# A layer with seven-product matrix pairs: the three fp32r passes of a product become the outer loop in every pair

## The chip, the cores and the metric

The kernel runs on one core of a Trainium2 chip. The metric is the device time of one execution in microseconds (us); three executions were timed. All tensors are fp32; a matmul reads its operands as fp32r (fp32 rounded to fewer bits), and a product of full width is built from three fp32r matmuls.

## The reference

One inference step of one layer on 512 prompt tokens and 8 sequences of 8 sample tokens (576 tokens, width 2048):

```python
h = rmsnorm(x, norm_g)
proj = h @ w_in          # merge gates ga, gb; conv inputs cB, cC, cx, cg; q, k, v, gg; rank-16 code
za = cB * causal_conv3(cC * cx) * silu(cg)
zb = head_rmsnorm(gated_linear_attention(q, k, v, code)) * silu(gg)
merged = sigmoid(ga) * (za @ w_branch_a) + sigmoid(gb) * (zb @ w_branch_b)
y = rmsnorm(x + merged @ w_out, final_norm_g)
```

Returned are y for prompt and samples, and the new states of the convolution and of the attention.

## The kernel before

**Two parts.** Up to about 703 us the kernel normalises x and does the k, q, v columns and the attention (its matmuls have line 1620). From there on all matmuls of line 1979 belong to 76 **pairs**. A pair is two 128-column tiles of weights against all 576 tokens and all 2048 rows, worked as a 2x2 block product with 7 sub-products instead of 8 (`PRODUCTS`, `NPROD` = 7): the blocks are a11, a12, a21, a22 of the weights and 288-token halves of the activations.

**The stages.** Pairs 0 to 51 (`FIRST`) are the columns of w_in that are left; pairs 52 to 59 (from `PAIR_A`) are w_branch_a, 60 to 67 (from `PAIR_B`) w_branch_b, 68 to 75 (from `PAIR_C`) w_out. The activation operands of the seven products are the same for all pairs of a stage. They lie in `SLOTS[stage]`: names y11, y12, y21, y22 are quarters of `act_y` (row k of a slot starts 1152 elements after row k - 1), numbers 0 to 3 are slots of `act_x` (row k starts 288 elements after row k - 1, right where row k - 1 ends). Products that read `act_x` are called x products here, the others y products. Stage 1 has four x products in a pair, A three, B four, C three.

**One product** is 8 rows k (`KH`) times 3 passes: 24 matmuls of 128 x 128 weights by 288 columns, added in one PSUM area. The passes (`PASSES`, line 471) are high weights by high activations (0, 0), high weights by low activations (0, 1), low weights by high activations (1, 0). ACT makes the high weights of product g (`split_hi`, line 1158, `ring_hi`, semaphore `part_hi`), DVE then subtracts them from the fp32 weights for the low ones (`split_lo`, line 2099, `ring_lo`, semaphore `part_lo`). Both run two products ahead, in a ring of three (`RING`). Before that, DVE forms the weight sums that four of the seven products need (`add_pieces`, line 2106). After a product ACT or DVE reads the PSUM area (`save`, line 1390, semaphore `part_saved`, and the stage functions such as `out_pair`).

**The order of matmuls** is written out in the PE part (lines 1927 to 1984). In the first pair of a stage (`late`: pairs 0, 52, 60, 68) the pass is the outer loop and k the inner, with passes in the order (0,0), (1,0), (0,1): the low activations are awaited last there, and `part_lo` in front of the second pass. In all other pairs k is the outer loop and the pass the inner, and PE waits for `part_lo` before the first matmul of the product:

```python
late = u in (0, PAIR_A, PAIR_B, PAIR_C)
if not late:
    pe.wait_ge(part_lo, g + 1)
order = [(n, k) for n in range(3) for k in range(KH)]
if not late:
    order = [(n, k) for k in range(KH) for n in range(3)]
```

In stage C PE also turns the finished tiles of the pair before (five transposes of line 1882 in front of products 1 and 3, `turn_out`).

**The end.** In the last pair the products run in `LAST_ORDER` = 0, 1, 2, 4, 5, 3, 6. `turn_early` (four transposes) stands in front of loop step (n, k) = (0, 3) of product 3, and `turn_first_late` (three) in front of (0, 5) of product 6; `turn_late` comes after everything. `turn_early` waits for the sums that DVE makes of products 4 and 5 (`out_pair`, lines 2800 and 2803), `turn_first_late` for that of product 3. DVE adds the turned tiles to the rows of x (`add_last`, line 2821), multiplies rows by the final norm weights (`weight`, line 2841; each call increments `weighted`), ACT squares them (`squares`, line 1453), both make the inverse root (`means`, `root_out`, `roots`), and `scale_row` on ACT (tiles 4 and 2) and DVE (tiles 3, 0, 1) scales the rows, which SP and POOL store. `EARLY` is tiles 3 and 4, `LATE` tiles 0 to 2.

Of the kernel before, what the change touches and what calls it, by code (L numbers as in the profile page):

```python
# [67 lines left out]
PAIRS_G, PAIRS_B, PAIRS_O = len(FIRST), 8, 8  # L68
# [27 lines left out]
def hybrid_kernel(nc, x_prompt, x_sample, state_conv, state_gla, norm_g, w_in, conv_w, w_alpha2,  # L96
# [51 lines left out]
    with ctx:  # L148
# [461 lines left out]
        def place(m):  # L610


            return (m + 1) % PLACES
# [502 lines left out]
        def _(act):  # L1116
# [348 lines left out]
            def save_c21(u):  # L1465

                act.wait_ge(prod_done, NPROD * u + NPROD)
                act.wait_ge(c11_read, u + 1)
                A(mix[u % 2][:, 1, 0:HALF], psum_of(u)[1], ACT.Copy, scale=-1.0).then_inc(c21_act, 1)
# [77 lines left out]
            def scale_row(t, count):  # L1547

                act.wait_ge(y_rstd, count)
                act.wait_ge(weighted, PAIRS_O - 1 + count)  # L1550
                if count == 1:
                    act.wait_ge(back_in, 16 * AWAY)
                for n, (_, part) in enumerate(parts_of_row(t)):
                    if n == 1 and count == 1:
                        save_c21(NPAIR - 1)
                    A(part, part, ACT.Copy, scale=stat[:, 24 + t:25 + t]).then_inc(y_act, 1)


# [12 lines left out]
        def _(pe):  # L1571
# [355 lines left out]
            for u in range(NPAIR):  # L1927
                f = phase_of(u)
                b1, b2, b3 = psum_of(u)
                for g in range(u * NPROD, (u + 1) * NPROD):  # L1930
                    p = product_at(g)
                    slot = SLOTS[f][p]
                    out = (b2, b3, b2, b1, b2, b3, b2)[p]

                    fresh = 0
                    if u == 0 and p in (1, 2, 4, 6):
                        fresh = (1, 2, 4, 6).index(p) + 1
                    if u in (PAIR_A, PAIR_B) and p in AHEAD[f - 1]:
                        pe.wait_ge(blk_in[p], 16 * (f + sum(p in AHEAD[n] for n in range(f))))
                    elif u in (PAIR_A, PAIR_B):  # L1940
                        fresh = split_count(f - 1, p)
                    if u == PAIR_C:
                        fresh = c_split(C_HI, p)
                        if p in SPLIT_WAY:
                            pe.wait_ge(blk_in[p], landed(p))
                    if fresh:
                        pe.wait_ge(x_hi, fresh)
                    if p == 0 and u < U_X and u % 16 == 15:
                        turn_tails(u // 16)
                    if u > PAIR_C and g % NPROD in (1, 3):  # L1950
                        turn_out(u - 1, g % NPROD // 2)
                    if p == 0 and u >= 2:
                        pe.wait_ge(*c21_done(u - 2))
                    if p == 1 and u >= 2:
                        pe.wait_ge(*c12_done(u - 2))
                    if p == 3 and u >= 2:
                        pe.wait_ge(c11_read, u - 1)
                    if p in (2, 4, 5, 6):
                        pe.wait_ge(part_saved, 4 * u + {2: 1, 4: 3, 5: 3, 6: 4}[p])
                    pe.wait_ge(part_hi, g + 1)  # L1960
                    r = g % RING

                    late = u in (0, PAIR_A, PAIR_B, PAIR_C)
                    if not late:
                        pe.wait_ge(part_lo, g + 1)
                    order = [(n, k) for n in range(3) for k in range(KH)]
                    if not late:
                        order = [(n, k) for k in range(KH) for n in range(3)]
                    for n, k in order:
                        if g == NG - 2 and (n, k) == (0, 3):  # L1970
                            turn_early()
                        if g == NG - 1 and (n, k) == (0, 5):
                            turn_first_late()
                        a, b = ((0, 0), (1, 0), (0, 1))[n] if late else PASSES[n]
                        if late and k == 0 and n == 1:
                            pe.wait_ge(part_lo, g + 1)
                        if late and k == 0 and n == 2 and fresh:
                            pe.wait_ge(x_lo, fresh)
                        mm = nc.tensor.matmul(out, (ring_hi, ring_lo)[a][r][:, k * P:(k + 1) * P],  # L1979
                                              slot_of(slot, b)[:, k, :],  # L1980
                                              start=(p in (0, 1, 3) and k == 0 and n == 0),
                                              stop=(k == KH - 1 and n == 2),
                                              skip_group_check=(p in (2, 4, 5, 6)))
                    mm.then_inc(prod_done, 1)
# [5 lines left out]
        def _(dve):  # L1990
# [855 lines left out]
            for u in range(NPAIR):  # L2846
                kind = kind_of(u)
                last = kind_of(u - 1) if u else "branch"
                for p in range(NPROD):
# [58 lines left out]
                    m = u - 1 - PAIR_C  # L2908
                    if m >= 0 and p in (1, 3):
                        add_rows(m, p // 2)  # L2910
                    if u == NPAIR - 1 and p == 5:
                        dve.wait_ge(x_row_in[place(L)], 64 * (L // PLACES + 1))
                        add_last(EARLY, 0, 2, acc[1][:, 0:4 * P], 2 * L + 1)
                    if m >= 0 and p == (6 if u < NPAIR - 1 else 5):
                        weight(m, range(NT + 1), m + 1)
                    if u == NPAIR - 1 and p == 5:
                        means(EARLY, PAIRS_O, L + 1)


            def roots(tiles, count):  # L2920

                dve.wait_ge(rms_out, count)
                refined(of_tiles(16, tiles), of_tiles(8, tiles), None, of_tiles(24, tiles), of_tiles(32, tiles))
                dve.sem_inc(y_rstd, 1)

            def scale_row(t, count):

                dve.wait_ge(weighted, L + count)
                inverse = stat[:, 24 + t:25 + t]
                for n, (_, part) in enumerate(parts_of_row(t)):  # L2930
                    at = place(L) if n == 2 else part.shape[1]
                    ins = V.tensor_scalar(part[:, 0:at], part[:, 0:at], inverse, None, ALU.mult)
                    if n == 2:
                        last = part[:, at, :]
                        ins = V.scalar_tensor_tensor(out=last, in0=last, scalar=inverse, in1=out_rows[:, at, OUT_N:],
                                                     op0=ALU.mult, op1=ALU.mult)
                    ins.then_inc(y_dve, 1)

            def last_squares():
# [6 lines left out]
                g = (L + 1) * (NT + 1) + LATE[0]  # L2946
                link(V.tensor_reduce(parts[:, g:g + len(LATE)], junk, AX_X, ALU.add))

            weight(L, [SCALED_BY_ACT[0]], L + 1)
            roots(EARLY, 1)  # L2950
            dve.wait_ge(back_in, 16 * AWAY)
            add_last(LATE, 0, 1, acc[1][:, 4 * P:7 * P], 2 * L + 2)
            scale_row(SCALED_BY_DVE[0], 1)
# [56 lines left out]
```

## Time and profile before

| what | us |
|---|---|
| median of 3 executions | 2437.24 (2436.47 to 2437.5) |
| the profiled execution, its own time | 2437.08 |
| its span, first to last instruction | 2435.3 |
| PE busy in the span | 2402.7 |
| DVE, ACT, POOL busy | 1875.7, 1089.0, 283.8 |
| granted TensorE clock, mean | 0.996 |

An execution takes 1.8 us more than the span between its first and last instruction. A row of a timeline has the start, the length, the engine, the line of the kernel, the operation with output and inputs, and how many like instructions are taken together; in brackets how long the engine sat idle before and what it waited for. A matmul's length is from its start to its end in the pipeline, so lengths overlap; the distance between two starts is what a matmul costs in a stream.

### The profile page before, as it was taken

To read this page: it belongs to the slowest core of one execution; us is meant where nothing else is said; L and a number is where in the kernel's file an instruction comes from. 1 tells how busy PE (TensorE), PEld (TensorE's weight loads), DVE (VectorE), ACT (ScalarE), POOL (GpSimd) and SP (SyncE) were. 2 spreads that over 40 slices of the span, in tenths; PEclk is the share of its full clock that TensorE was granted. 3 is DMA by queue.
4 is the path that set the end of the run, shared out by engine and by line. 5 is a ranking of instruction groups with operands and counts; after the bars stand their busy time and mean duration, and the time that the engine had idled before them with its cause. 6 is when DMAs were issued, how large, how long until landed. Compare 5 with 4: busy or idle time off the path is not lost.

```text
span 2435.3 us, 43889 instructions
## 1 busy us (share of the span) xinstructions
PE 2402.7 (99%) x18015; PEld 2362.1 (97%) x18015; DVE 1875.7 (77%) x2765; ACT 1089.0 (45%) x1654; POOL 283.8 (12%) x493
## 2 busy tenths in 40 slices
PE   9999999999999999999999999999999999999996
PEld 7999999999999999999999999999999999999996
DVE  7467777676788878878878788876678778989776
ACT  5353444444443444444344344444445445445443
POOL 4002121120200000010000011000000110332111
PEclk9999999999999999999999999999999999999998
DMA  7325444353633334433443455554578768669555
GB/s 212 82 67 178 116 135 137 108 179 91 193 101 104 104 105 104 121 97 96 122 116 85 122 155 154 158 153 129 165 203 288 221 214 290 199 191 297 153 155 162
DMA packets 456248, 369.02 MB, mean 152 GB/s; under 512 B 15989, under 2 KB 425761, under 8 KB 453537
## 3 DMA queue, kind: packets, MB, share of 16 engines
q1 hardware_dynamic: 419826, 238.91, 35.7%
q0 software_dynamic: 36224, 127.32, 15.9%
q8 instruction: 143, 2.34, 0.4%
q14 instruction: 55, 0.45, 0.1%
HBM read 286.50 MB, written 79.68 MB: 150 GB/s over the span
## 4 chain that ended last, share of the span: by engine, by line
PE 93%; DVE 3%; DMA 2%; issue 1%; ACT 1%; SPq 0%; DVEq 0%; ACTq 0%
PE bank L1979 37%; PE acc L1979 29%; PE acc L1620 20%; PE acc L1713 1%; PE acc L1782 1%; PE bank L1776 1%; DVE ring_lo L2103 1%; DMA x_rows<-in_x_prompt 1%; PE bank L1740 1%; PE bank L1752 1%; PE bank L1773 1%; DMA x_f<-zw_d 1%; DMA pa<-in_w_branch_a 0%; PE bank L1695 0%; PE acc L1882 0%
## 5 line engine op out<-in xcount | busy, mean ns | idle before, releaser
L2103 DVE TENSOR_TENSOR ring_lo<-pa,ring_hi 128x1024 fp32r<-128x1024 f32 x532 | 650.0, 1222 | 201.8 <-ACT ring_hi L1168 198.8
L1168 ACT ACTIVATE ring_hi<-pa 128x1024 fp32r<-128x1024 f32 x532 | 561.6, 1056 | 386.1 <-PE bank L1979 220.3
L1620 PE MATMUL acc<-act_y,w_hi 128*128 128x288 f32 x2560 | 514.8, 297 | 0.1
L1979 PE MATMUL bank<-act_y,ring_hi 128*128 128x288 f32 x2432 | 478.2, 295 | 2.0 <-DVE act_y L2784 1.1
L1979 PE MATMUL bank<-act_x,ring_hi 128*128 128x288 f32 x2432 | 475.6, 294 | 1.6 <-ACT act_x L1451 1.4
L1979 PE MATMUL acc<-act_x,ring_hi 128*128 128x288 f32 x2176 | 435.4, 294 | 0.2 <-DVE ring_lo L2103 0.2
L1620 PEld LDWEIGHTS acc<-act_y,w_hi 128*128 128x128 f32 x2560 | 411.6, 189 | 3.4 <-ACT mix_tile L1183 0.5
L1979 PEld LDWEIGHTS bank<-act_x,ring_hi 128*128 128x128 f32 x2432 | 387.5, 189 | 2.3 <-ACT act_x L1451 1.8
L1979 PEld LDWEIGHTS bank<-act_y,ring_hi 128*128 128x128 f32 x2432 | 385.1, 189 | 3.1 <-DVE act_y L2784 1.6
L1620 PE MATMUL acc<-act_y,w_lo 128*128 128x288 f32 x1280 | 375.5, 295 | 0.0
L1979 PEld LDWEIGHTS acc<-act_x,ring_hi 128*128 128x128 f32 x2176 | 351.1, 189 | 0.7 <-issue 0.4
L1979 PE MATMUL bank<-act_x,ring_lo 128*128 128x288 f32 x1216 | 344.5, 296 | 0.1
L1979 PE MATMUL bank<-act_y,ring_lo 128*128 128x288 f32 x1216 | 343.1, 295 | 0.0
L1979 PE MATMUL acc<-act_x,ring_lo 128*128 128x288 f32 x1088 | 322.3, 296 | 0.0
L1979 PE MATMUL acc<-act_y,ring_hi 128*128 128x288 f32 x1472 | 295.6, 295 | 2.5 <-DVE ring_lo L2103 2.5
L1620 PEld LDWEIGHTS acc<-act_y,w_lo 128*128 128x128 f32 x1280 | 240.8, 189 | 0.0
L1979 PEld LDWEIGHTS acc<-act_y,ring_hi 128*128 128x128 f32 x1472 | 236.1, 189 | 3.4 <-issue 3.4
L1979 PEld LDWEIGHTS bank<-act_y,ring_lo 128*128 128x128 f32 x1216 | 223.2, 188 | 0.3 <-DVE ring_lo L2103 0.2
L1979 PEld LDWEIGHTS bank<-act_x,ring_lo 128*128 128x128 f32 x1216 | 222.7, 188 | 0.4 <-DVE ring_lo L2103 0.3
L1979 PE MATMUL acc<-act_y,ring_lo 128*128 128x288 f32 x736 | 217.1, 295 | 0.0
L1979 PEld LDWEIGHTS acc<-act_x,ring_lo 128*128 128x128 f32 x1088 | 204.1, 188 | 0.0
L1393 ACT ACTIVATE part<-acc 128x288 f32<-128x288 f32 x152 | 62.4, 410 | 265.1 <-PE acc L1979 265.0
(405 smaller groups left out, 2743.4 us busy)
## 6 DMA issues: line engine op xcount, KB each, us to landing
pa<-in_w_in SPq DMA_DIRECT2D x208, 512.0 KB, 5.3
raw<-in_w_in SPq DMA_DIRECT2D x40, 1024.0 KB, 5.7
pa<-in_w_branch_a SPq DMA_DIRECT2D x32, 512.0 KB, 6.0
pa<-in_w_branch_b SPq DMA_DIRECT2D x32, 512.0 KB, 7.0
pa<-in_w_out SPq DMA_DIRECT2D x32, 512.0 KB, 6.9
states<-in_state_gla POOLq DMA_DIRECT2D x48, 256.0 KB, 3.3
out<-states POOLq DMA_DIRECT2D x48, 256.0 KB, 3.0
zt_d<-gate_tile POOLq DMA_DIRECT2D x12, 576.0 KB, 3.5
```

The lines of the kernel that those rows point to most:

```text
L1168: A(ring_hi[g % RING][:, :], piece_of[src][u % 2][:, :], ACT.Copy).then_inc(part_hi, 1)
L1393: A(dst[:, :], psum_of(u)[b], ACT.Copy).then_inc(part_saved, 1)
L1620: return nc.tensor.matmul(half_bank[h % 2][:, 0:HALF], (w_hi, w_lo)[a][u % 2][:, k * P:(k + 1) * P], y_of(k, b, j), start=(k == 0 and n == ...
L1713: mm = nc.tensor.matmul(b_gram[:, a * P:(a + 1) * P], dec[:, kk, a * P:(a + 1) * P], dec[:, kk, MID + a * P:MID + (a + 1) * P], start=(kk ...
L1740: nc.tensor.matmul(b_smp[r:r + TS // 2, :], q_pad[:, a % 2, kk, b, :], state_of(2 * a + b)[:, kk, :], start=(a == 0), stop=(a == NS // 2 - 1))
L1752: mm = nc.tensor.matmul(bank[:, kk, :], kd_one[:, kk * P:(kk + 1) * P], v2[:, j // (NS // 2), :], start=True, stop=True)
L1773: nc.tensor.matmul(out, v_rows[:, b, v * P:(v + 1) * P], scores[:, b * P:(b + 1) * P], start=True, stop=(c == 0))
L1776: nc.tensor.matmul(out, s_prompt[:, kk, v * P:(v + 1) * P], qe[:, kk, b * P:(b + 1) * P], start=False, stop=(kk == KK - 1))
L1782: mm = nc.tensor.matmul(b_chunk[kk], k, v[:, :], start=(n == 0), stop=(n == 2))
L1979: mm = nc.tensor.matmul(out, (ring_hi, ring_lo)[a][r][:, k * P:(k + 1) * P], slot_of(slot, b)[:, k, :], start=(p in (0, 1, 3) and k == 0 a ...
L2103: V.tensor_tensor(ring_lo[g % RING][:, :], piece_of[source_of(g)][u % 2][:, :], ring_hi[g % RING][:, :].bitcast(F32), ALU.subtract).then_i ...
```

## The change

The pairs that aren't the first of a stage get the loops of the first pairs, but with the passes in the order (0,0), (0,1), (1,0), and wait for `part_lo` only in front of the third pass. At the end, the multiplication of the last-but-one pair's rows by the norm weights is split into tiles 0 to 2 before the last addition of the early tiles, and tiles 3 and 4 behind it; ACT awaits the norm weights only in front of the third part of a row; and `roots` and `weight` of tile 4 change places.

```diff
@@ scale_row on ACT
                 act.wait_ge(y_rstd, count)
-                act.wait_ge(weighted, PAIRS_O - 1 + count)
                 if count == 1:
                     act.wait_ge(back_in, 16 * AWAY)
                 for n, (_, part) in enumerate(parts_of_row(t)):
                     if n == 1 and count == 1:
                         save_c21(NPAIR - 1)
+                    if n == 2:
+                        act.wait_ge(weighted, PAIRS_O + count)
@@ the order of matmuls on PE
                     late = u in (0, PAIR_A, PAIR_B, PAIR_C)
-                    if not late:
+                    second = not late
+                    if not late and not second:
                         pe.wait_ge(part_lo, g + 1)
                     order = [(n, k) for n in range(3) for k in range(KH)]
-                    if not late:
+                    if not late and not second:
                         order = [(n, k) for k in range(KH) for n in range(3)]
                     for n, k in order:
@@
-                        if late and k == 0 and n == 1:
+                        if k == 0 and (late and n == 1 or second and n == 2):
                             pe.wait_ge(part_lo, g + 1)
@@ the end on DVE
+                    if m >= 0 and p == 6 and u < NPAIR - 1:
+                        weight(m, range(NT + 1), m + 1)
                     if u == NPAIR - 1 and p == 5:
+                        weight(m, LATE, m + 1)
                         dve.wait_ge(x_row_in[place(L)], 64 * (L // PLACES + 1))
                         add_last(EARLY, 0, 2, acc[1][:, 0:4 * P], 2 * L + 1)
-                    if m >= 0 and p == (6 if u < NPAIR - 1 else 5):
-                        weight(m, range(NT + 1), m + 1)
-                    if u == NPAIR - 1 and p == 5:
+                        weight(m, EARLY, m + 1)
                         means(EARLY, PAIRS_O, L + 1)
@@ scale_row on DVE
-                dve.wait_ge(weighted, L + count)
+                dve.wait_ge(weighted, PAIRS_O + count)
@@
+            roots(EARLY, 1)
             weight(L, [SCALED_BY_ACT[0]], L + 1)
-            roots(EARLY, 1)
```

## Rows read from the trace of the kernel before

**Rows 1.** The page: chain that ended last, share of the span by engine.

```profile
PE 93%; DVE 3%; DMA 2%; issue 1%; ACT 1%; SPq 0%; DVEq 0%; ACTq 0%
```

**Rows 2.** The chain of waits: start, length, what; whole pairs 0, 2 and 54.

```profile
703.48 22.35 PE bank L1979 x168
...
748.08 22.25 PE bank L1979 x168
...
1907.86 22.24 PE bank L1979 x168
```

**Rows 3.** Timeline of PE, end of pair 0 and beginning of pair 1.

```profile
722.47 1.23 PE L1979 MATMUL bank<-act_x,ring_hi 128*128 128x288 f32 x8
...
724.61 1.23 PE L1979 MATMUL bank<-act_x,ring_hi 128*128 128x288 f32 x8
725.67 0.42 PE L1979 MATMUL acc<-act_y,ring_hi 128*128 128x288 f32 x2
...
728.87 0.43 PE L1979 MATMUL acc<-act_x,ring_hi 128*128 128x288 f32 x2
...
735.21 0.42 PE L1979 MATMUL bank<-act_y,ring_hi 128*128 128x288 f32 x2
```

**Rows 4.** Timeline of PE: first matmuls of pair 52 and of pair 53.

```profile
1862.02 1.22 PE L1979 MATMUL bank<-act_y,ring_hi 128*128 128x288 f32 x8
...
1884.33 0.42 PE L1979 MATMUL acc<-act_y,ring_hi 128*128 128x288 f32 x2
```

**Rows 5.** Timeline of PE: first matmuls behind a wait, in pairs 53, 61, 62, 69.

```profile
1888.55 0.50 PE L1979 MATMUL acc<-act_y,ring_hi 128*128 128x288 f32 x2 [0.90 <-DVE ring_lo L2103]
...
2064.49 0.51 PE L1979 MATMUL acc<-act_x,ring_hi 128*128 128x288 f32 x2 [0.18 <-DVE ring_lo L2103]
...
2069.25 0.51 PE L1979 MATMUL acc<-act_y,ring_hi 128*128 128x288 f32 x2 [1.34 <-DVE ring_lo L2103]
...
2072.70 0.50 PE L1979 MATMUL acc<-act_y,ring_hi 128*128 128x288 f32 x2
...
2094.89 0.29 PE L1979 MATMUL bank<-act_y,ring_lo 128*128 128x288 f32 x1
2095.14 0.51 PE L1979 MATMUL bank<-act_y,ring_hi 128*128 128x288 f32 x2
...
2250.76 0.50 PE L1979 MATMUL acc<-act_y,ring_hi 128*128 128x288 f32 x2 [0.27 <-DVE ring_lo L2103]
```

**Rows 6.** Timeline of ACT and DVE around the waits of pairs 53 and 61.

```profile
1885.30 1.06 ACT L1168 ACTIVATE ring_hi<-pa 128x1024 fp32r<-128x1024 f32 x1 [5.77 <-DVE pa L2113]
...
2070.72 0.39 ACT L1393 ACTIVATE part<-acc 128x288 f32<-128x288 f32 x1
...
2071.34 1.22 DVE L2103 TENSOR_TENSOR ring_lo<-pa,ring_hi 128x1024 fp32r<-128x1024 f32 x1
```

**Rows 7.** Timeline of PE in the last two products and behind them.

```profile
2408.14 0.42 PE L1979 MATMUL bank<-act_y,ring_hi 128*128 128x288 f32 x2
...
2409.34 0.60 PE L1882 MATMUL acc<-ident,mix_tile 128*128 128x128 f32 x4
...
2413.78 0.49 PE L1882 MATMUL acc<-ident,mix_tile 128*128 128x128 f32 x3
...
2416.06 0.52 PE L1882 MATMUL bank<-ident,mix_tile 128*128 128x128 f32 x3 [0.59 <-ACT mix_tile L1469]
```

**Rows 8.** Timeline of DVE and ACT in the same stretch.

```profile
2408.41 0.46 DVE L2803 TENSOR_TENSOR mix_tile<-acc,part 128x288 f32<-128x288 f32 x1 [0.63 <-PE acc L1979]
...
2410.65 1.49 DVE L2841 TENSOR_TENSOR out_rows<-out_rows 128x1280 f32<-128x1280 f32 x1
...
2412.34 0.46 DVE L2803 TENSOR_TENSOR mix_tile<-bank,part 128x288 f32<-128x288 f32 x1
...
2416.68 0.55 DVE L2821 TENSOR_TENSOR out_rows<-out_rows,bank 128x384 f32<-128x384 f32 x1
...
2415.50 0.41 ACT L1469 ACTIVATE mix_tile<-acc 128x288 f32<-128x288 f32 x1 [0.47 <-PE acc L1979]
```

## The prediction

> **What bounds the kernel.** I read the page first: PE is busy for 2402.7 of 2435.3 us at a mean granted clock of 0.996 (table above), and it holds 93% of the chain that ended last [rows 1]. So a change of the matmul order counts in two ways only: through the pace of the stream itself, and through the moments in which the stream stops. The chain of waits, read pair by pair, gives the pace: a pair in the middle of stage 1 takes 22.25 us, one of stage A 22.24 [rows 2]. 168 matmuls in 22.25 us are 132.4 ns each, without a gap. The timeline of PE at the borders of stages gives the stops, and those of ACT and DVE what ends them. Last comes the end of the kernel, where PE, DVE and ACT hand work to each other in a chain.
>
> **What the new order costs in the stream.** The kernel before already runs the loops that the change brings, in the first pair of each stage. Pair 0 takes 22.35 us, pair 2 takes 22.25 [rows 2]; pair 0 has no stop in it. The difference lies in the x products. The last one of pair 0 runs from 722.47 to 725.67, 3.20 us; two of pair 1 run from 728.87 to 735.21, 6.34 us, 3.17 each [rows 3]. The y product at the start of pair 1 takes 3.20 us (725.67 to 728.87), as y products of that slot do in either order. The trace doesn't say why an x product is slower when k is the inner loop. What differs is that each matmul then reads the row right behind the one before, where the old order reads rows of the same k in both planes. It can't be the pass: the last x product of pair 0 takes 1.07 us for each of its first two passes and 1.06 for the third [rows 3]. The new order has the same three passes, high by high, high by low, low by high, only the last two changed in place; so I take the whole price of pair 0. The wait in front of a later pass costs nothing that can be seen there, when it is met.
>
> - Stage 1: pairs 1 to 51, 51 times (22.35 - 22.25) = 5.1 us.
> - Stage A: pair 52 runs from 1862.02 to 1884.33, 22.31 us [rows 4], pair 54 takes 22.24 [rows 2]: 7 times 0.07 = 0.5 us.
> - Stages B and C: their first pairs are full of other stops, so I take 0.10 us for four x products, 0.025 each. B has 7 times 4 of them, 0.7 us; C has 7 times 3, 0.5 us.
>
> Together +6.8 us. From below, the price could be 0, if pair 0 is slow for a reason of its own; from above, 0.03 us for each of the 274 x products, 8.2 us. I take the measured pairs, because pair 52, in another stage and with other engines at other work, shows the same.
>
> [...]
>
> **What the later wait gives back.** PE stops for the low weights in non-first pairs at a few places. A product's third pass begins 16 matmuls, 2.1 us, after its start, and the low weights can be that much later. A matmul is 0.30 us long and its successor starts 0.13 after it, so a stop is the idle time in the row plus 0.17.
>
> - Pair 53, product 1, starts at 1888.55. The product before starts at 1884.33 [rows 4] and takes 3.16 us (22.24 us less what the other six take), so it could start at 1887.49. The high weights are there at 1885.30 + 1.06 = 1886.36 [rows 6]. Gain 1.06 (the 0.90 idle plus 0.17), and 0.07 more as the first matmuls behind a stop are stretched (0.50 against 0.43 [rows 3, 5]): 1.1 us.
> - Pair 61: product 0 starts at 2064.49, product 1 at 2069.25, product 2 at 2072.70 [rows 5]. Without the first stop (0.18 + 0.17 = 0.35) product 0 starts at 2064.14, product 1 3.20 us later at 2067.34, product 2 could at 2070.50. But product 2 also waits for ACT to save product 0's sum, which ends at 2070.72 + 0.39 = 2071.11 [rows 6], set by ACT and DVE work that doesn't follow PE. So it starts near 2071.15 instead of 2072.70. Its low weights are ready at 2071.34 + 1.22 = 2072.56 [rows 6], needed at 2073.3. Gain 1.6 us with the stretch. **Next late** is this save, then nothing: DVE's queue is full there and doesn't get earlier, but it has 2.1 us more room.
> - Pair 62, product 2, starts at 2095.14, 0.25 after the matmul before it in place of 0.13, and is stretched [rows 5]: 0.2 us.
> - Pair 69, product 0, 2250.76: 0.27 + 0.17, and the stretch [rows 5]: 0.5 us.
>
> Together -3.4 us. Stops inside the first pairs stay, since these pairs don't change. Bounds: nothing, if something else holds PE to the same moment, and 4.0 us if the save doesn't hold it either. Queued behind the moved wait is the low pass alone; nobody but the reader of the finished product waits for it, and the product ends no later than before.
>
> **The end.** `turn_early` stands in front of loop step (0, 3), `turn_first_late` in front of (0, 5). In the old order these are the 10th and the 16th matmul, in the new one the 4th and the 6th, so the transposes move forward by 0.8 and 1.3 us, and what they need doesn't. Product 3 starts at 2408.14; PE is at `turn_early` at 2408.54 instead of 2409.34. DVE's sum of product 5 ends at 2408.41 + 0.46 = 2408.87 [rows 7, 8]; from an ACT result to the transpose behind it took 0.15 us (2415.91 to 2416.06 [rows 7, 8]). So PE stops from 2408.54 to about 2409.0: 0.45 us. `turn_first_late` would come about 0.1 us before its sum. These are PE's stops before the last product ends, and from there on the chain goes PE, ACT (2415.50), PE (2416.06), DVE (2416.68) with no room [rows 7, 8]. So +0.5 us. DVE's work moves well: 768 of the 1280 columns of the 1.49 us multiplication go in front of the addition of the early tiles, where DVE waits for `turn_early` since 2408.87, and the means and roots follow sooner, but that is the early tiles' branch, and the late tiles end last. I cost the split, one more DVE instruction, the swap of `roots` and the later wait on ACT at nothing: idle DVE and the wait for turned tiles hide them; if that cover were gone, some 0.1 us. Bounds: -0.3 (DVE's first late addition starts sooner and nothing stops PE) and +0.7.
>
> **Sum:** 6.8 - 3.4 + 0.5 = +3.9 us on the profiled execution's 2437.08, 2441.0. The median is 0.16 above that execution: **2441.1 us, 0.16% more**. A measurement of this kernel can tell about 0.2% (4.9 us) from no change, so this is a forecast of "no difference that can be told", leaning to slower.
>
> **Rivals.**
>
> 1. **The order is free.** Pair 0 is slower for its place, not its loops; then -3.4 + 0.5 = -2.9: 2434.3. For it: only 2 undisturbed first pairs exist. Against: they agree, product by product, and only x products differ. [...] Chance 0.12.
> 2. **The stops don't come back (slower).** In pair 61 DVE and ACT set the pace; if product 2 and those behind it are held at the old moments by ACT's saves or by weight sums that come out of DVE's queue, the 1.8 us of pairs 61 and 62 are lost: +5.7, 2442.9, already over the 0.2%. It decides once the low weights of a product come more than 2.1 us after its start, or a save more than 1.5 us later than I read. If pairs 53 and 69 give nothing either, +7.3: 2444.5. For it: DVE runs without a pause there. Against: high weights are finished a whole DVE instruction before low ones. Chance 0.12.
> 3. **The change does little.** PE is never short of low weights in the steady pairs, so without a price and with stops that only move, 2437.2. Chance 0.05.
>
> My forecast has 0.68; its own range is 2439.4 to 2442.9, from the bounds of x price and tail. The last 0.03 is for something faster that I don't see.
>
> **How the numbers follow.** Slower by over 0.2% begins at 2442.1: a fifth of my forecast and rival 2, 0.25. Faster by over 0.2% is below 2432.4: 0.04. The rest, 0.71, is within. The range, 2437.0 to 2443.8, holds my case, rival 3 and rival 2 up to its first price, and leaves out rival 1.
>
> **What the profile would show.** Right: pairs of stage 1 at 22.35 us (22.34) in place of 22.25, x products of 3.20 us, y products unchanged; product 1 of pair 53 without a stop; product 2 of pair 61 behind an ACT save; no wait of PE for `ring_lo` outside first pairs; a stop of 0.4 to 0.5 us in front of `turn_early`; the span longer by 3 to 5 us. Wrong: pairs of stage 1 at 22.25 or above 22.4, or stops in them at the third pass.

## The result, and the profile after

The changed kernel takes **2441.21 us** (median of 20 runs, 2439.62 to 2444.25); the kernel before, measured beside it, 2436.68 (20 runs). The ratio is 1.0018, with a 95% interval of 1.0011 to 1.0024: slower, and with the ratio itself just inside the 0.2% that the forecast counted as no difference (the interval reaches beyond it). The profiled execution took 2441.34 us, with a span of 2439.6 at a mean granted clock of 0.997.

The page, with busy time of the engines and the shares of the chain that ended last, answers [rows 1] and the table of before:

```profile
PE 2408.9 (99%) x18015; PEld 2368.7 (97%) x18015; DVE 1876.1 (77%) x2766; ACT 1088.8 (45%) x1654; POOL 283.8 (12%) x493
PE 93%; DVE 3%; DMA 2%; issue 1%; ACT 0%; POOL 0%; SPq 0%; DVEq 0%; ACTq 0%; POOLq 0%
```

The chain of waits, with start and length of each step, answers [rows 2] (whole pairs 0, 2 and 54):

```profile
703.82 22.35 PE bank L1981 x168
...
748.52 22.35 PE bank L1981 x168
...
1912.22 22.31 PE bank L1981 x168
```

PE issues the same 18015 matmuls, yet is busy 6.2 us longer, and the span is 4.3 us longer. So PE idles less than before and streams more slowly. Pair 0 still takes 22.35 us. The difference is that pair 2 now takes as long.

The timeline of PE (start, length, line, operands, count of matmuls merged in the row) shows both halves. The first five rows are starts of products in pair 1; below them are the first matmul of pair 52, product boundaries in pairs 53, 61 and 62, and the first matmul of stages B and C (pairs 60 and 68, the rows at 2045.94 and 2226.57). They answer [rows 3 to 5].

```profile
726.01 2.29 PE L1981 MATMUL acc<-act_y,ring_hi 128*128 128x288 f32 x16
...
729.21 2.30 PE L1981 MATMUL acc<-act_x,ring_hi 128*128 128x288 f32 x16
...
732.41 2.29 PE L1981 MATMUL acc<-act_x,ring_hi 128*128 128x288 f32 x16
...
735.61 2.30 PE L1981 MATMUL bank<-act_y,ring_hi 128*128 128x288 f32 x16
...
742.01 2.26 PE L1981 MATMUL acc<-act_y,ring_hi 128*128 128x288 f32 x16
...
1867.43 0.43 PE L1981 MATMUL bank<-act_y,ring_hi 128*128 128x288 f32 x2
...
1889.75 2.27 PE L1981 MATMUL acc<-act_y,ring_hi 128*128 128x288 f32 x16
...
1892.91 1.37 PE L1981 MATMUL acc<-act_y,ring_hi 128*128 128x288 f32 x9
...
2045.94 0.30 PE L1981 MATMUL bank<-act_x,ring_hi 128*128 128x288 f32 x1
...
2068.91 2.29 PE L1981 MATMUL acc<-act_x,ring_hi 128*128 128x288 f32 x16
...
2072.11 2.26 PE L1981 MATMUL acc<-act_y,ring_hi 128*128 128x288 f32 x16
...
2075.94 0.80 PE L1981 MATMUL acc<-act_y,ring_hi 128*128 128x288 f32 x4 [0.51 <-ACT part L1393]
...
2097.34 1.22 PE L1981 MATMUL bank<-act_y,ring_lo 128*128 128x288 f32 x8
2098.70 1.07 PE L1981 MATMUL bank<-act_y,ring_hi 128*128 128x288 f32 x6
...
2226.57 0.29 PE L1981 MATMUL bank<-act_y,ring_hi 128*128 128x288 f32 x1
```

The two x products of pair 1 start at 729.21 and 732.41, and the y product behind them at 735.61: 3.20 us each, where [rows 3] has 3.17. The y product that starts the pair takes 3.20 as before. The one at 742.01 takes 3.15: not all y products are alike, and that turned out to be the thread to pull. In pair 53 (from 1889.75) product 1 follows product 0 without a stop. In pair 61 product 1 does too (2072.11), and product 2 waits, for ACT. In pair 62 product 2 starts at 2098.70, 0.31 us after it could: the row before it begins at 2097.34 and its 8 matmuls take 1.05 us at the pace around them. In the list of idle engine waits there is no wait of PE for `ring_lo` any more outside the first pairs.

The starts of the stages give the ledger. "Before" is the same matmul in the kernel before: 703.32 for pair 0, 1862.02 for pair 52 [rows 4], 2041.13 and 2222.40 for pairs 60 and 68, 2408.14 for the last product but one [rows 7].

| stretch | before, start | after, start | grew by | forecast |
|---|---|---|---|---|
| in front of pair 0, code unchanged | 703.32 | 703.66 | +0.34 | 0 |
| stage 1 | 1862.02 | 1867.43 | +5.07 | +5.1 |
| stage A | 2041.13 | 2045.94 | -0.60 | +0.5 - 1.1 |
| stage B | 2222.40 | 2226.57 | -0.64 | +0.7 - 1.8 |
| stage C to the last product but one | 2408.14 | 2411.96 | -0.36 | +0.5 - 0.5 |
| from there to DVE's last scaling of rows | 2423.53 | 2427.92 | +0.57 | +0.5 |
| sum | | | +4.38 | +3.9 |

Each start stands for the end of its row's stretch. The +0.34 lies in code that both kernels share, so the stretches with changed code made 4.04. What comes behind DVE's last scaling, mostly stores, takes 11.64 us against 11.75 before, so the whole span grew by 4.28.

The timeline of ACT behind the stops of pairs 61 and 62, which answers [rows 6]:

```profile
2075.14 0.44 ACT L1431 ACTIVATE gate_r<-mix_tile 128x288 fp32r<-128x288 f32 x1 [1.31 <-DVE y_f L2741]
2075.49 0.39 ACT L1393 ACTIVATE part<-acc 128x288 f32<-128x288 f32 x1
...
2098.26 0.39 ACT L1393 ACTIVATE part<-bank 128x288 f32<-128x288 f32 x1
```

And that of DVE in pair 62:

```profile
2092.93 0.46 DVE L2712 TENSOR_TENSOR part<-acc,part 128x288 f32<-128x288 f32 x1 [2.33 <-DMA mix_tile<-ma_d]
```

The save of pair 61 ends at 2075.49 + 0.39 = 2075.88 and product 2 starts at 2075.94, where it could have started at 2072.11 + 3.16 = 2075.27: a stop of 0.67. In pair 62 ACT again saves last, until 2098.65. It was held up by a slice of `gate_r` at 2097.91, whose input DVE made late, because DVE had stood for 2.33 us in front of L2712 for a transfer of `mix_tile` (0.86 us in the kernel before).

At the end of the kernel, the timeline of PE answers [rows 7]:

```profile
2411.96 0.30 PE L1981 MATMUL bank<-act_y,ring_hi 128*128 128x288 f32 x1
...
2412.79 0.63 PE L1883 MATMUL acc<-ident,mix_tile 128*128 128x128 f32 x4 [0.27 <-issue]
...
2420.51 0.52 PE L1883 MATMUL bank<-ident,mix_tile 128*128 128x128 f32 x3 [0.59 <-ACT mix_tile L1469]
```

And that of DVE answers [rows 8]:

```profile
2412.23 0.46 DVE L2805 TENSOR_TENSOR mix_tile<-acc,part 128x288 f32<-128x288 f32 x1 [0.66 <-PE acc L1981]
2412.61 0.95 DVE L2843 TENSOR_TENSOR out_rows<-out_rows 128x768 f32<-128x768 f32 x1
...
2414.13 0.68 DVE L2843 TENSOR_TENSOR out_rows<-out_rows 128x512 f32<-128x512 f32 x1
...
2427.92 0.48 DVE L2938 SCALAR_TENSOR_TENSOR out_rows<-out_rows,stat 128x256 f32<-128x256 f32 x1
```

The sum that `turn_early` turns is done at 2412.69. PE has issued the three matmuls in front of it by 2412.36 (2411.96 and three times 0.133) and starts the transposes at 2412.79: 0.43 us of standing. From `turn_late` (2420.51) to the start of DVE's last scaling it is 7.41 us, against 7.47 before (2416.06 to 2423.53). The 1.49 us multiplication [rows 8] has become 0.95 and 0.68, and nothing behind the last transposes has moved for it.

### The profile page after: what moved, and what is told of

Read it like the earlier page. It is cut to its first block, busy times and chain, and to the rows that moved or that the text cites. A ratio compares the mean times of both kernels' runs of the same rounds, so it can differ in the third digit from the quotient of the medians.

```text
span 2439.6 us, 43886 instructions
## 1 busy us (share of the span) xinstructions
PE 2408.9 (99%) x18015; PEld 2368.7 (97%) x18015; DVE 1876.1 (77%) x2766; ACT 1088.8 (45%) x1654; POOL 283.8 (12%) x493
## 4 chain that ended last, share of the span: by engine, by line
PE 93%; DVE 3%; DMA 2%; issue 1%; ACT 0%; POOL 0%; SPq 0%; DVEq 0%; ACTq 0%; POOLq 0%
PE bank L1981 38%; PE acc L1981 29%; PE acc L1621 20%; PE acc L1714 1%; PE acc L1783 1%; PE bank L1777 1%; DMA x_rows<-in_x_prompt 1%; PE bank L1753 1%; PE bank L1741 1%; PE bank L1774 1%; DMA x_f<-zw_d 1%; DVE ring_lo L2105 0%; PE bank L1696 0%; PE acc L1883 0%; PE acc L1805 0%
## 5 line engine op out<-in xcount | busy, mean ns | idle before, releaser
L1981 PE MATMUL bank<-act_y,ring_hi 128*128 128x288 f32 x2432 | 350.5, 296 | 2.1 <-DVE act_y L2786 1.1
L1981 PE MATMUL bank<-act_x,ring_hi 128*128 128x288 f32 x2432 | 351.0, 296 | 1.2 <-ACT act_x L1451 1.0
L1981 PEld LDWEIGHTS bank<-act_x,ring_hi 128*128 128x128 f32 x2432 | 333.3, 188 | 1.9 <-ACT act_x L1451 1.4
L1981 PEld LDWEIGHTS bank<-act_y,ring_hi 128*128 128x128 f32 x2432 | 331.6, 189 | 3.2 <-DVE act_y L2786 1.6
L1981 PE MATMUL acc<-act_x,ring_hi 128*128 128x288 f32 x2176 | 312.4, 296 | 0.0
L1981 PE MATMUL acc<-act_y,ring_hi 128*128 128x288 f32 x1472 | 210.2, 295 | 0.5 <-ACT part L1393 0.5
L1981 PE MATMUL bank<-act_x,ring_lo 128*128 128x288 f32 x1216 | 186.8, 296 | 0.1
L1981 PE MATMUL bank<-act_y,ring_lo 128*128 128x288 f32 x1216 | 186.4, 296 | 0.0
L1393 ACT ACTIVATE part<-bank 128x288 f32<-128x288 f32 x152 | 62.2, 410 | 244.4 <-PE bank L1981 244.0
L1981 PE MATMUL acc<-act_x,ring_lo 128*128 128x288 f32 x1088 | 167.0, 296 | 0.0
```

The source lines that it names most:

```text
L1393: A(dst[:, :], psum_of(u)[b], ACT.Copy).then_inc(part_saved, 1)
```

## The experiments

Two questions were open. Do the parts of the sum hold when each is undone alone (first and fourth run)? And why is an x product slower with `k` as the inner loop (all the others)? The prediction had taken that price from pair 0 without a cause. All runs start from the changed kernel; times are compared with runs of the kernel before on the same chip.

### The wait in front of the first pass

```diff
-                    if not late and not second:
+                    if not late:
                         pe.wait_ge(part_lo, g + 1)
@@
-                        if k == 0 and (late and n == 1 or second and n == 2):
+                        if late and k == 0 and n == 1:
```

> The loops of the change, but the low weights awaited in front of the first pass again. My theory (the later wait returns 3.4 us at the stops of pairs 53, 61, 62 and 69, and has no part in the price): pairs of stage 1 stay at 22.35 us; product 1 of pair 53 stops for about 1.1 us again and product 1 of pair 61 for 1.5; 3 us slower than the change, about 2444.5 against 2436.7 of before, a ratio of 1.003. Rival (the wait in the middle of a product is itself what slows the stream): pairs of stage 1 go back to 22.25 us and the time to about 2438.

Measured: 2444.27 us (8 runs) against 2437.11, ratio 1.003 (1.0019 to 1.0041). Pairs of stage 1 take 22.35 us. The chain of waits:

```profile
748.37 22.35 PE bank L1981 x168
```

The timeline of PE in pairs 53 and 61:

```profile
1893.70 0.77 PE L1981 MATMUL acc<-act_y,ring_hi 128*128 128x288 f32 x4 [0.78 <-DVE ring_lo L2105]
...
2074.87 1.30 PE L1981 MATMUL acc<-act_y,ring_hi 128*128 128x288 f32 x8 [1.32 <-DVE ring_lo L2105]
```

The stops are back where [rows 5] has them: 0.94 in pair 53, then 0.34, 1.48 and 0.18 at products 0, 1 and 2 of pair 61, each with some 0.08 more because the first matmuls behind it are stretched. The stop of 0.43 us in front of pair 69 is back too. By stages this run is longer than the changed kernel by 1.01 us in A, 1.34 in B and 0.38 in C, 2.7 together. The two profiled executions differ by 2443.92 - 2441.34 = 2.6, the ratios by 0.12%, 2.9 us. So the later wait is worth 2.6 to 2.9 us, somewhat less than the 3.4 that were forecast, and moving it does nothing to the pace of a pair.

### Rows that don't lie right behind each other

The prediction named what differs in an x product of pair 0: each matmul reads the row right behind the one before.

```diff
+                    if second:
+                        order = [(n, k) for n in range(3) for k in (0, 2, 4, 6, 1, 3, 5, 7)]
```

> The change with the rows k of each pass in the order 0, 2, 4, 6, 1, 3, 5, 7 in all but the first pairs, so that no matmul reads the row of act_x right behind the one before. Theory A (an x product is slower where each matmul's moving row begins where the last one's ended): x products at 3.17 us or less, pairs of stage 1 at 22.25 or less, time about 6.8 us under the change, 2434.4, ratio to before 0.999. Theory B (the old order gains because it loads the same high weights twice in a row): nothing changes, pairs 22.35 us, time 2441.2. Theory C (what counts is the distance between the starts of two rows, whatever it is): x products take a third value.

Measured: 2441.81 us (10 runs), ratio 1.0019 (1.001 to 1.0029); pairs of 22.36 us in the chain of waits, x products of 3.195 to 3.200 in stage 1.

```profile
748.09 22.36 PE bank L1983 x168
```

That theory falls: with every other row the x products are as slow as with neighbours.

### The two high passes row by row, the low one behind them

```diff
+                    if second:
+                        order = [(n, k) for k in range(KH) for n in range(2)] + [(2, k) for k in range(KH)]
```

> The first two passes (high weights by high and by low activations) with k as the outer loop again, the low weights alone in a third pass. 16 of the 24 matmuls then come in twos with the same weights and the same row in two planes. Theory B (same weights twice) and theory A (same row in two planes) both expect most of the 0.028 us of an x product back: 3.175 to 3.185 us, pairs of stage 1 at 22.26 to 22.30, time 2436 to 2438, with the stops of pairs 53, 61 and 69 still gone. If the price is tied to the pass being the outer loop at all, x products stay at 3.20.

Measured: **2435.91 us** (10 runs) against 2437.11, ratio 0.9995 (0.9985 to 1.0004). The chain of waits:

```profile
748.63 22.28 PE bank L1983 x168
```

The timeline of PE in pair 1 and in pair 61:

```profile
729.38 2.28 PE L1983 MATMUL acc<-act_x,ring_hi 128*128 128x288 f32 x16
...
732.56 2.27 PE L1983 MATMUL acc<-act_x,ring_hi 128*128 128x288 f32 x16
...
2072.32 2.40 PE L1983 MATMUL acc<-act_y,ring_hi 128*128 128x288 f32 x16 [0.51 <-ACT part L1393]
```

The x product from 729.38 to 732.56 takes 3.18 us (the last x product of a pair stays at 3.198), and a pair 22.28: two thirds of the price are gone, while the low weights are still awaited 2.1 us into the product. Product 1 of pair 61 doesn't stop, product 2 waits for ACT's save as in the changed kernel. In this order the same weights are loaded twice in succession, and the two planes of the same row of `act_x` are read in succession. Either could be what speeds x products up, and the two runs behind the next one were to tell.

### The transposes where they were

```diff
-                        if g == NG - 2 and (n, k) == (0, 3):
+                        if g == NG - 2 and (n, k) == (1, 1):
@@
-                        if g == NG - 1 and (n, k) == (0, 5):
+                        if g == NG - 1 and (n, k) == (1, 7):
```

> The change with the early and the first late transposes behind as many matmuls as before the change (9 and 15). My theory: the stop in front of the four transposes (0.46 us more than before in the change's trace) and the one of 0.17 in front of the three go, and the stretch from the start of the last-but-one product to the end is 0.5 us shorter; in the time that is within the scatter. Rival (the end is set by DVE's early branch): DVE ends no earlier relative to that start.

Measured (one run): 2441.25 us. The timeline of PE at the end:

```profile
2412.15 1.36 PE L1981 MATMUL bank<-act_y,ring_hi 128*128 128x288 f32 x9
...
2413.35 0.60 PE L1883 MATMUL acc<-ident,mix_tile 128*128 128x128 f32 x4
```

And DVE's last scaling of rows in it:

```profile
2427.54 0.48 DVE L2938 SCALAR_TENSOR_TENSOR out_rows<-out_rows,stat 128x256 f32<-128x256 f32 x1
```

From the last product but one to DVE's last scaling it is 2427.54 - 2412.15 = 15.39 us, exactly that of the kernel before (2423.53 - 2408.14) and 0.57 less than in the changed kernel, with the split multiplication and the other edits at the end still in. So the transposes' place makes all of the tail's loss, and with the transposes in their old place those edits are worth nothing in either direction. Whether they save something behind the transposes' new place stays open: no run takes them out. The other traces agree: 15.94 us in the run with the wait in front, whose transposes stand in the new place, and 15.39 in the two runs below that have the old loops in the last pair. The total doesn't show it: here pair 68, whose length varies from kernel to kernel, took 28.8 us in place of 27.6.

### Low weights between the two high passes

The old loop, `k` outside, with passes high by high, low by high, high by low: the same weights never come twice in succession, the same row of the activations still does.

```diff
-                    if not late and not second:
+                    if not late:
                         order = [(n, k) for k in range(KH) for n in range(3)]
@@
-                        a, b = ((0, 0), (1, 0), (0, 1))[n] if late else PASSES[n]
+                        a, b = ((0, 0), (1, 0), (0, 1))[n]
```

The wait is put in front of the product again, as in the first run.

> k as the outer loop as before the change, low weights awaited first, but in each row the passes high by high, low by high, high by low: no two matmuls in a row load the same weights, while the first two of each row read the same row of the same plane and the third reads that row in the other plane. Theory B (the old pace comes from loading the same weights twice): x products 3.20 us, pairs of stage 1 at 22.35. Theory A2 (it comes from reading the same row, or the same row in the other plane of act_x, again): x products 3.17, pairs 22.25.

Measured (one run): 2436.84 us against 2437.42. In the chain:

```profile
748.39 22.25 PE bank L1981 x168
```

Three of the x products take 3.172 to 3.174 us and the last one 3.180, and every interval of pair 1 has the length that it has in the kernel before, to 0.001 us. So it doesn't matter whether the same weights come twice in succession. What this run has in common with the kernel before is that all three matmuls of a row k stand together, and that the row's two planes change places in the sequence makes no difference.

### The same weights twice, on another row

```diff
                                               slot_of(slot, b)[:, k, :],
+                                              slot_of(slot, b)[:, (k + (second and n == 1)) % KH, :],
```

This comes on top of the order of the third run and takes the place of the line above it. The second pass then multiplies another row, so this kernel sums other terms.

> The order of the run with the high passes by row, but the second matmul of each row reads the low activations of the row behind (so the second pass multiplies weights by another row's activations: part of the sums is another one). The same weights come twice in a row, no row twice. Theory B: x products 3.17 to 3.185 us as in that run, pairs of stage 1 at 22.28. Theory A2: x products 3.20, pairs 22.35.

Measured (one run): 2435.88 us; pairs of stage 1 take 22.28 us in the chain, their four x products 3.174, 3.192, 3.174 and 3.199 us.

This run tells less than it was meant to. Its second matmul of step k reads row k + 1, and so does the first of step k + 1: the same row still comes twice in succession. So the 22.28 decides nothing between the two theories, and the verdict on the weights rests on the run before it.

### Rows four apart

```diff
+                    if second:
+                        order = [(n, k) for n in range(3) for k in (0, 4, 1, 5, 2, 6, 3, 7)]
```

> The loops of the change with rows 0, 4, 1, 5, 2, 6, 3, 7 in each pass. Every other step is 4608 bytes instead of 1152 or 2304. If rows that begin at the same place within 512 bytes count as the same for the pace, x products fall to about 3.185 us; if only the very same row does, they stay at 3.20, as with every other row (3.195 to 3.200 measured). I expect 3.20.

Measured (one run): 2439.79 us; pairs of stage 1 take 22.33 in the chain.

```profile
748.22 22.33 PE bank L1981 x168
```

The timeline of PE, an x product of pair 1 and the same one of pair 2, each with the start of the product behind it:

```profile
732.18 2.27 PE L1981 MATMUL acc<-act_x,ring_hi 128*128 128x288 f32 x16
...
735.34 2.30 PE L1981 MATMUL bank<-act_y,ring_hi 128*128 128x288 f32 x16
...
754.44 2.30 PE L1981 MATMUL bank<-act_x,ring_hi 128*128 128x288 f32 x16
...
757.64 2.30 PE L1981 MATMUL bank<-act_y,ring_hi 128*128 128x288 f32 x16
```

The expectation was only partly met. Most x products are at 3.183 or 3.200 us, but three in pair 1 and two in most pairs of stage C take 3.160 to 3.168, without a row ever coming twice in succession. So "the same row twice" isn't the rule either. And the order of the rows isn't all of it: the product that starts at 732.18 takes 3.16 us, the one at 754.44 takes 3.20, and the two read the same rows at the same places in the same order. Pair 7, with the weights in the same part of the ring and the sum in the same PSUM area as in pair 1, takes 3.20 for it too. Something else, perhaps how the matmuls before them ran, has a part in the pace. No run isolates it.

### The new order only in the four pairs that stop

If the order costs and the later wait gives, each can be had where it pays.

```diff
-                    second = not late
+                    second = u in (PAIR_A + 1, PAIR_B + 1, PAIR_B + 2, PAIR_C + 1)
@@
+                    if second:
+                        order = [(n, k) for k in range(KH) for n in range(2)] + [(2, k) for k in range(KH)]
```

> The old loops in all pairs but 53, 61, 62 and 69, which run the two high passes by row and the low weights in a third pass, awaited there; the end with the transposes where the old loops have them. If price and return are what I read (0.1 us a pair against 3.2 us in all, 0.5 us of stop at the end), pairs of stage 1 take 22.25, the stops at pairs 53 and 69 are gone, and the time is 3.3 us under before: 2433.6 against 2436.9, ratio 0.9986. Rival (the return depends on all pairs having the later wait): 2435.5 or more.

Measured: **2434.70 us** (11 runs, 2432.09 to 2437.93) against 2437.42, ratio 0.999 (0.9981 to 0.9999). The chain of waits:

```profile
748.32 22.25 PE bank L1983 x168
```

The timeline of PE in pairs 53 and 61:

```profile
1887.73 2.30 PE L1983 MATMUL acc<-act_y,ring_hi 128*128 128x288 f32 x16
...
2070.28 2.40 PE L1983 MATMUL acc<-act_y,ring_hi 128*128 128x288 f32 x16 [0.51 <-ACT part L1393]
```

Stage 1 keeps its 22.25 us. Product 1 of pair 53 starts at 1887.73 in place of 1888.55 [rows 5], product 2 of pair 61 at 2070.28 in place of 2072.70. The 3.3 us that were expected came out as 2.7. It is faster than the kernel before, by an interval that just leaves out 1, and its median is 6.5 us under that of the changed kernel.

### The activations 128 bytes further down

In pair 1 of the changed kernel y products that read the first 288 tokens take 3.194 and 3.202 us, the one that reads the last 288 takes 3.153. If the place in SBUF decides that, moving `act_y` and `act_x` must change who is slow.

```diff
-        parts = put("parts", [P, (PAIRS_O + 1) * (NT + 1)], F32)
+        put("shift", [P, 16], F32)
@@
+        parts = nc.alloc_sbuf_tensor_at("parts", [P, (PAIRS_O + 1) * (NT + 1)], F32, offset=g_at + 4 * QUARTER + 2 * P * 4)
```

> The change with act_y and act_x starting 128 bytes lower in each partition (parts goes behind them), nothing else. In all traces so far the y products on the first 288 tokens (y11, y21) take 3.195 to 3.204 us and those on the last 288 (y12, y22), whose rows start 1152 bytes on, so at the other half of a 256-byte step, take 3.153 to 3.160, in either loop order. Theory M (the pace hangs on where in SBUF the moving rows start, 133.3 ns at one half of 256 bytes, 131.4 at the other, and for act_x on how these follow each other): y11 and y21 fall to 3.153 to 3.160 and y22 and y12 rise to 3.20; x products, whose rows start at all multiples of 128, stay near 3.20; pairs of stage 1 take 22.31 instead of 22.35. Rival (it hangs on the tokens, the PSUM area or the product's place in the pair): nothing moves.

Measured (one run): 2443.18 us; the part in front of pair 0 ended 1.3 us later and pair 68 took 29.1 us, so the total says little. The timeline of PE in pair 1:

```profile
727.27 2.28 PE L1983 MATMUL acc<-act_y,ring_hi 128*128 128x288 f32 x16
...
730.44 2.29 PE L1983 MATMUL acc<-act_x,ring_hi 128*128 128x288 f32 x16
...
743.21 2.29 PE L1983 MATMUL acc<-act_y,ring_hi 128*128 128x288 f32 x16
...
746.41 2.30 PE L1983 MATMUL acc<-act_x,ring_hi 128*128 128x288 f32 x16
```

The y product on the first half, 727.27 to 730.44, now takes 3.17 us (3.195 before the shift), and the one on the last half, 743.21 to 746.41, takes 3.20 (3.153). The halves changed places, with PE's instructions the same but for the addresses of the rows that they read. So the place in SBUF has a part in the pace. x products stay at 3.20. A pair takes 22.33 us, 0.014 less than before the shift, where 22.31 was expected: the direction is right, the size about a third, since the first half fell only to 3.167 and not to 3.153. The places of the weights and of the PSUM areas didn't change. Other tensors that share the memory of `act_y` and `act_x`, such as `out_rows`, moved with them, but PE reads none of them in pair 1.

### Both

> The kernel with the later wait only in pairs 53, 61, 62 and 69, and the activations 128 bytes lower. By theory M pairs of stage 1 take 22.25 - 0.04 = 22.21 us (two y products faster, one slower), those of stage B likewise; A and C have as many of either kind and stay. 52 + 8 pairs times 0.04 is 2.4 us: 2432.3 against 2437, ratio 0.998. Rival: no different from the kernel without the shift, ratio 0.999.

The edit is the two before it together. Measured: **2433.29 us** (11 runs, 2432.17 to 2437.08) against 2436.68, ratio 0.9987 (0.9978 to 0.9996). In the chain:

```profile
748.88 22.23 PE bank L1985 x168
```

Pairs of stage 1 take 22.227 us in place of 22.247, half of what was expected; over 51 pairs that is 1.0 us. It is the fastest version, 0.13% below the kernel before. Its lead over the version without the shift is within the scatter of the two; what is shown is the pace in the profile.

## Why the prediction was right

**The price of the order** was forecast at 5.1 us for stage 1 and came out at 5.07: pair 0 was a true sample of what the loops cost, in this stage and in the others. A pair grew by 0.100 us in stage 1 (22.247 to 22.347), by 0.073 in stage A, 0.100 in stage B and 0.079 in stage C, where 0.10, 0.07, 0.10 and 0.075 had been taken. Taking the price from code that already ran the loops was the step that carried the forecast. The y products weren't quite unchanged: in stage 1 one of them grew by 0.007 us and one shrank by as much. The cause that the prediction left open isn't the one it leaned to: neighbouring rows don't make it, since every other row costs as much. Nor is it the repeated load of the same weights, nor the place of the wait. The order in which the rows are read brings the price and takes it away (22.347, 22.360, 22.333, 22.280 and 22.247 us a pair in five orders), and the rows' place in SBUF has a part in the pace. Why they do isn't shown, and the run with rows four apart shows that the two together don't fix the pace.

**Rival 1**, the free order, is refuted by the pairs of 22.35 us: the trace has 131.4 ns (3.153 us by 24) and 133.3 ns (3.200 by 24) for matmuls of one shape at one clock, so the pace isn't set by the number of columns alone. The Trainium skill ("TensorE: Matmul & The Clock Gate", section "Back-to-back issue gap") gives columns by 2.4 GHz plus 2.5 ns, for 288 columns an estimate of 122.5 ns, as the gap of an isolated matmul, and says that in a stream of weight loads and matmuls both set the spacing. So that formula doesn't speak for this stream, and its own size isn't tested here.

**What the later wait gives back.** Pair 53: no stop, as forecast, and stage A closes at -0.60, the sum of its two terms. Pair 61: the next late thing is ACT's save, with a stop of 0.67 where 0.65 (2071.15 less 2070.50) was forecast. Rival 2 is refuted there. **Pair 62 is the miss.** The forecast had its stop vanish; it grew instead, to 0.31 + 0.10, and stage B gained 0.64 instead of 1.1. The step that failed is "then nothing": it took the save in pair 61 to be the last thing in the way because DVE's queue is full. PE was in product 2 of pair 61 already 30.00 us after the start of stage B (2075.94 - 2045.94), where it had been 31.57 (2072.70 - 2041.13), and met in pair 62 a chain that doesn't follow PE: DVE waits for the DMA of `mix_tile`, ACT's `gate_r` slice for DVE, the save for ACT, product 2 for the save. Of the 1.8 us taken for pairs 61 and 62 about 0.5 were lost so in this execution. But the loss doesn't always come with the change. In the run with every other row PE is in product 2 of pair 61 just as early (29.98 us after the start of stage B), DVE waits 1.87 us for `mix_tile` instead of 2.33, and product 2 of pair 62 follows without a stop. Its timelines of DVE and of PE:

```profile
2092.71 0.46 DVE L2714 TENSOR_TENSOR part<-acc,part 128x288 f32<-128x288 f32 x1 [1.87 <-DMA mix_tile<-ma_d]
```

```profile
2095.49 2.27 PE L1983 MATMUL bank<-act_y,ring_hi 128*128 128x288 f32 x16
...
2098.65 1.63 PE L1983 MATMUL bank<-act_y,ring_hi 128*128 128x288 f32 x11
```

The sum behind that wait begins 46.5 us after the start of stage B here, 47.0 in the changed kernel. With rows four apart and with the order in four pairs alone it begins after 45.2 and 45.3 us, and pair 62 has no stop; with the transposes put back after 47.1, and the stop is 0.47 + 0.10. So whether PE stops there goes by when that transfer lands, and this differs between the traces; why it does stays open. Pair 69's stop vanished as forecast (0.43 us). Stage C came out 0.36 better than forecast, because a stop in pair 68, before any of its changed pairs, was 0.4 shorter; PE waits there for `act_x` from ACT, and pair 68 varies from 27.5 to 29.1 us between the kernels measured, so this isn't credited to the change.

**The end** was forecast at +0.5 and came out at +0.57: the stop before `turn_early` grew by 0.46 us (0.45 forecast), that before `turn_first_late` by 0.17 (0.1). The run with the transposes put back took all of it away. It also shows that the split multiplication, the later wait on ACT and the swap of `roots` are worth nothing with the transposes in their old place; in the new place they weren't tested alone.

The total, +4.26 us between the profiled executions against +3.9, hides an error of 0.5 in stage B behind one of 0.36 with the other sign in stage C, and contains 0.34 us from a part that nobody changed. The median hides another: 2441.1 was forecast and 2441.21 measured, but the forecast counted from 2437.24, the median of three executions, where twenty gave 2436.68. The difference of the medians is 4.5 us against 3.9. That the times agree to 0.1 us is luck; that the terms agree is not.

## What to carry to other kernels

When code of the new kind already runs somewhere in the kernel before, time it product by product there: that one pair gave 5.1 us where 5.07 was measured, though nobody knew the cause. A later wait that costs a slower order is to be used only where the wait ever stops the engine; here that is 4 of 76 pairs in the trace of before, and doing so turned 4.5 us of loss into 2.7 us of gain. Such places can move: in the last version pairs 63 and 64, outside the four, each took 0.3 us more than the pairs behind them. When a stop is removed, follow PE to the next pairs too, and ask which transfers don't come earlier with it.

## What was not expected of the hardware

Matmuls of one shape, at one granted clock and without a gap, run here at paces from 131.4 ns (products of 3.153 us) to 133.4 ns (3.202). Each product's length repeats from pair to pair: pairs 1 to 51 of the changed kernel take 22.346 or 22.347 us, but for pairs 14, 15, 30 and 31, lengthened by transposes in front of pairs 15 and 31. Moving the activations by 128 bytes swapped the pace of the two halves of the y products (3.195 and 3.153 us became 3.167 and 3.200). For x products the sequence of rows decides (3.171 to 3.180 us with all matmuls of a row together, 3.200 with row after row, 3.160 to 3.200 with rows four apart). For y products it matters less: the one that starts a pair of stage 1 takes 3.194 us with row after row and 3.204 with every other row. The same rows in the same order don't always give the same pace: 3.16 us in pair 1 and 3.20 in pair 2 with rows four apart. Which boundary in SBUF stands behind it, and what is carried over from one product to the next, stays open: no run moved `act_x` or `act_y` alone, or by another distance.

Two things cost nothing where a cost had to be reckoned with: loading other weights between two uses of the same (22.25 us either way), and a semaphore wait in the middle of a product that is already met (22.347 us a pair with it, and with the wait in front of the product).
